# Block ends of a two-layer SSM and attention stack, worked by half rows instead of whole rows

## The reference, cut to what matters

```python
def rmsnorm(x, g):
    y = x32 * lax.rsqrt(jnp.mean(x32 * x32, axis=-1, keepdims=True) + EPS)
    return (y * g).astype(x.dtype)
...
    x = x + rmsnorm(h, mix_post_g[i])          # h: output of the block's last product
    u = rmsnorm(x, mem_pre_g[i])               # u: input of the next block
```

## Time and profile before

| | |
|---|---|
| time, median of 3 runs | 965.77 us (965.77 to 967.42) |
| the profiled execution's own time | 968.91 us |
| its span | 967.1 us |
| TensorE busy | 929.4 us (96%) |
| VectorE busy | 563.3 us (58%) |
| ScalarE busy | 487.8 us (50%) |
| mean granted TensorE clock | 0.987 |

### The profile page before, as it was taken

How to read it: one execution, slowest core, us unless ns; L and a number is a source line. 1 busy time by engine, 2 the same in 40 slices (tenths; PEclk the granted TensorE clock), 3 DMA queues, 4 the chain that set the end, 5 groups by cost and what they waited for, 6 DMA issues and landing times.

```text
span 967.1 us, 15638 instructions
## 1 busy us (share of the span) xinstructions
PE 929.4 (96%) x6624; PEld 860.2 (89%) x6624; DVE 563.3 (58%) x645; ACT 487.8 (50%) x670; POOL 36.1 (4%) x51
## 2 busy tenths in 40 slices
PE   7999999998999989999999999999999599999996
PEld 6999988787899889999988899987998499999885
DVE  6788465784565575455544854675755645554543
ACT  5566467764545564344433554665645534434332
POOL 1000001130000000000000220000000000000000
PEclk9999999999999999999999999999999799999999
DMA  8766442234653365555555697433643345555551
GB/s 261 260 187 192 145 153 89 88 127 138 204 188 128 127 209 187 173 174 186 189 190 189 218 266 220 132 131 131 217 138 115 119 143 191 188 174 174 197 194 44
DMA packets 121061, 163.80 MB, mean 169 GB/s; under 512 B 4076, under 2 KB 106916, under 8 KB 121012
## 3 DMA queue, kind: packets, MB, share of 16 engines
q1 hardware_dynamic: 117684, 151.99, 48.0%
q0 software_dynamic: 3328, 11.10, 3.7%
HBM read 162.01 MB, written 1.07 MB: 169 GB/s over the span
## 4 chain that ended last, share of the span: by engine, by line
PE 84%; DVE 10%; ACT 4%; issue 2%; DMA 1%; SPq 0%; DVEq 0%; ACTq 0%
PE bank L443 76%; DVE w_lo L1152 2%; DVE ntmp L1215 1%; PE bank L750 1%; PE bank L721 1%; DVE x L1218 1%; DVE ntmp L1194 1%; ACT ntmp L861 1%; PE bank L639 1%; PE bank L545 1%; DMA pre_row<-in_mix_pre_g_dram 1%; DVE stats L1183 1%; DVE stats L1185 1%; PE bank L805 1%; PE bank L677 0%
## 5 line engine op out<-in xcount | busy, mean ns | idle before, releaser
L1152 DVE TENSOR_TENSOR w_lo<-w_raw,w_hi 128x2048 fp32r<-128x2048 f32 x135 | 308.4, 2290 | 219.4 <-ACT w_hi L839 219.2
L443 PE MATMUL bank<-actT_hi,w_hi 128*128 128x256 f32 x1280 | 364.8, 285 | 4.8 <-DVE w_lo L1163 1.7
L443 PE MATMUL bank<-actT_lo,w_hi 128*128 128x256 f32 x1280 | 363.2, 284 | 0.0
L443 PE MATMUL bank<-actT_hi,w_lo 128*128 128x256 f32 x1280 | 363.1, 284 | 0.0
L839 ACT ACTIVATE w_hi<-w_raw 128x2048 fp32r<-128x2048 f32 x135 | 256.6, 1907 | 98.6 <-DMA w_raw<-in_ffn_w_down_dram 52.9
L443 PEld LDWEIGHTS bank<-actT_hi,w_hi 128*128 128x128 f32 x1280 | 246.7, 193 | 6.8 <-issue 4.6
L443 PEld LDWEIGHTS bank<-actT_lo,w_hi 128*128 128x128 f32 x1280 | 246.8, 193 | 0.1
L443 PEld LDWEIGHTS bank<-actT_hi,w_lo 128*128 128x128 f32 x1280 | 246.7, 193 | 0.0
L443 PE MATMUL bank<-w_hi,hT_hi 128*128 128x512 f32 x176 | 68.5, 389 | 0.0
L443 PE MATMUL bank<-w_lo,hT_hi 128*128 128x512 f32 x176 | 68.5, 389 | 0.0
L443 PE MATMUL bank<-w_hi,hT_lo 128*128 128x512 f32 x176 | 68.5, 389 | 0.0
(11 more groups left out here) (209 smaller groups left out, 1280.5 us busy)
## 6 DMA issues: line engine op xcount, KB each, us to landing
w_raw<-in_ffn_w_gu_dram SPq DMA_DIRECT2D x44, 1024.0 KB, 5.0
w_raw<-in_ffn_w_down_dram SPq DMA_DIRECT2D x22, 1024.0 KB, 4.9
w_raw<-in_ssm_w_in_dram SPq DMA_DIRECT2D x20, 1024.0 KB, 5.3
w_raw<-in_mem_w_kv_dram SPq DMA_DIRECT2D x16, 1024.0 KB, 5.6
w_raw<-in_ssm_w_out_dram SPq DMA_DIRECT2D x8, 1024.0 KB, 4.9
w_raw<-in_mem_w_q_dram SPq DMA_DIRECT2D x8, 1024.0 KB, 5.1
w_raw<-in_mem_w_o_dram SPq DMA_DIRECT2D x8, 1024.0 KB, 4.9
w_raw<-in_w_kv_dram SPq DMA_DIRECT2D x8, 1024.0 KB, 5.6
```

The source lines that it names most:

```text
L443: ins = pe.matmul(dst, a, b, start=first and n == 0, stop=last and n == len(passes) - 1, skip_group_check=True)
L1152: dve.tensor_tensor(lo[:, s, :], raw[:, s, :], hi[:, s, :].bitcast(F32), ALU.subtract).then_inc(w_lo_done, 1)
```

## The change

- **Last product.** The last two units are run by quarters: for each row tile, for each column half, both units' matmuls of that half (12 matmuls). `m_quarter` is raised after each of the first three quarters, `w_used` of both units only within the fourth.
- **Statistics.** `statistic_halves` squares each half when it is there, with a sum of its own; the first sum goes through one more small activation (scale by 1/1024, plus eps), and Ln takes it as its bias. For x the halves are waited for one by one. `w_hi` of unit `last` + 3 now stands behind all four statistics.
- **Update.** h times the gain row is formed by halves ahead of the norm (`gains`, from the bank), one before and one after the second half's sum. Then one operation for each half gives x = h·gain × norm + x. The two whole-row operations L1215 and L1218 are gone.
- **Next norm and transposes.** `normalise` writes two halves, TensorE waits for each half on its own. This holds for the first turn and the memory's turn too.
- **Weights on VectorE.** `w_lo` of unit `last` + 2 stands after the update of t = 1 instead of t = 0; that of `last` + 3 stands in `turn`, between the two row tiles.
- **Output.** Each half row tile is stored by a DMA of its own (four instead of two).

```diff
             def m_part(name, act_hi, act_lo, ready, last_y=None):
...
+                for t in range(ST):
+                    for half in range(2):
+                        for i in (n - 2, n - 1):
+                            if t == 0 and half == 0:
+                                ready(i)
+                                pe.wait_ge(w_lo_done, U[(name, i)] + 1)
+                            for r in range(MR):
+                                ins = part(i, t, half, r)
+                            if t and half:
+                                ins.then_inc(w_used, 1)
+                        if not (t and half):
+                            ins.then_inc(m_quarter, 1)
...
-                    pe.wait_ge(u_ready, 2 * k + t + 1)
                     for half in range(2):
+                        pe.wait_ge(u_ready, 4 * k + 2 * t + half + 1)
...
+            def statistic_halves(c, t, src, first, second):
+
+                for half, (s, count) in enumerate((first, second)):
+                    cols = slice(half * 512, half * 512 + 512)
+                    act.wait_ge(s, count)
+                    act.activation(ntmp[:, t, cols], src[:, cols], ACT.Square,
+                                   accum_out=stats[:, 0 if half else 6, c:c + 1]).then_inc(sum_ready, 1)
+                    act.wait_ge(sum_ready, sums_in(c, half))
+                    if half == 0:
+                        own.mark(act.activation(stats[:, 7, c:c + 1], stats[:, 6, c:c + 1], ACT.Identity, bias=eps_col, scale=1.0 / D))
+                own.wait()
+                own.mark(act.activation(stats[:, 1, c:c + 1], stats[:, 0, c:c + 1], ACT.Ln, bias=stats[:, 7, c:c + 1], scale=1.0 / D))
+                own.wait()
+                act.activation(stats[:, 2, c:c + 1], stats[:, 1, c:c + 1], ACT.Exp, scale=-0.5).then_inc(stat_ready, 1)
...
-                statistic(stat_col(n, 1, 0), 1, msum[1])
+                statistic_halves(stat_col(n, 1, 0), 1, msum[1], (m_quarter, 3 * n + 3), (w_used, last + 1))
+                if POST_TURN[n] is not None:
+                    statistic_halves(stat_col(n, 1, 1), 1, x[:, 1, :], (x_ready, 4 * n + 3), (x_ready, 4 * n + 4))
                 hi_upto(units_ahead(n))
...
+                    own.mark(dve.tensor_scalar(v0, total0, -0.5 / D, -0.5 * EPS, ALU.mult, ALU.add))
+                    if gains:
+                        gains(0)
+                    dve.wait_ge(sum_ready, sums_in(c, 1))
+                    own.wait()
+                    own.mark(dve.tensor_scalar(v, total, -0.5 / D, v0, ALU.mult, ALU.add))
+                    if gains:
+                        gains(1)
...
+            def turn(k, dst_hi, dst_lo, ahead=-1):
                 for t in range(ST):
+                    if t:
+                        lo_upto(ahead)
                     for half in range(2):
...
-                    own.mark(dve.scalar_tensor_tensor(out=ntmp[:, t, :], in0=msum[t], scalar=stats[:, 5, c:c + 1],
-                                                      in1=post_row[:], op0=ALU.mult, op1=ALU.mult))
-                    own.wait()
-                    dve.tensor_tensor(x[:, t, :], x[:, t, :], ntmp[:, t, :], ALU.add).then_inc(x_ready, 1)
-                    if units_ahead(n) > last_unit(M_OF_POST[n]) + 2:
-                        lo_upto(units_ahead(n) if t else last_unit(M_OF_POST[n]) + 2)
...
+                        own.mark(dve.tensor_tensor(ntmp[:, t, cols], bank[:, 4 + 2 * t + half, :], post_row[:, cols], ALU.mult))
...
+                        dve.scalar_tensor_tensor(out=x[:, t, cols], in0=ntmp[:, t, cols], scalar=stats[:, 5, c:c + 1],
+                                                 in1=x[:, t, cols], op0=ALU.mult, op1=ALU.add).then_inc(x_ready, 1)
+                    if t and units_ahead(n) > last_unit(M_OF_POST[n]) + 2:
+                        lo_upto(last_unit(M_OF_POST[n]) + 2)
```

More of the change, by code:

```diff
@@ L335, in stat_col, with sums_in @@
             return 4 + 4 * n + (2 * t + after if POST_TURN[n] is not None else t)
+        def sums_in(c, half):
+            return c + 1 if c < 4 else 2 * (c - 4) + 5 + half
         def last_unit(name):
@@ L510, in m_part @@
                 n = last_unit(name) - U[(name, 0)] + 1
[L512 to L531, removed]
@@ new lines, in part @@
+                def part(i, t, half, r):
+                    u, k = U[(name, i)], i * MR + r
+                    ah, al = act_hi[:, k, t * P:(t + 1) * P], act_lo[:, k, t * P:(t + 1) * P]
+                    cols = slice(r * D + half * 512, r * D + half * 512 + 512)
+                    wh, wl = hi[:, u % SLOTS, cols], lo[:, u % SLOTS, cols]
+                    return product(bank[:, 4 + 2 * t + half, :], [(ah, wh), (ah, wl), (al, wh)], k == 0, k == n * MR - 1)
+                for i in range(n - 2):
+                    ready(i)
+                    pe.wait_ge(w_lo_done, U[(name, i)] + 1)
+                    for t in range(ST):
+                        if t and i == 0 and last_y:
+                            last_y()
+                        for r in range(MR):
+                            for half in range(2):
+                                ins = part(i, t, half, r)
+                    ins.then_inc(w_used, 1)
@@ L1174, in tiles, with inverse_rms @@
                 return bank[:, b, :].rearrange("p (c n) -> p c n", n=S)
[L1176 to L1180, removed]
+            def inverse_rms(c, gains=None):
+                total, _, r, v, step, result, total0, _, v0 = [stats[:, n, c:c + 1] for n in range(9)]
+                dve.wait_ge(sum_ready, sums_in(c, 0))
+                if c < 4:
+                    own.mark(dve.tensor_scalar(v, total, -0.5 / D, -0.5 * EPS, ALU.mult, ALU.add))
+                else:
+                    own.mark(dve.tensor_scalar(v0, total0, -0.5 / D, -0.5 * EPS, ALU.mult, ALU.add))
[6 more added lines that the diff above has]
+                        gains(1)
                 own.wait()
@@ L1193, in normalise @@
                     dve.wait_ge(*((pre_loaded, 16 * k) if k else (pre_first, 16)))
-                dve.scalar_tensor_tensor(out=ntmp[:, t, :], in0=src[:, t, :], scalar=stats[:, 5, c:c + 1],
-                                         in1=pre_row[:], op0=ALU.mult, op1=ALU.mult).then_inc(u_ready, 1)
-            def turn(k, dst_hi, dst_lo):
+                for half in range(2):
+                    cols = slice(half * 512, half * 512 + 512)
+                    dve.scalar_tensor_tensor(out=ntmp[:, t, cols], in0=src[:, t, cols], scalar=stats[:, 5, c:c + 1],
+                                             in1=pre_row[:, cols], op0=ALU.mult, op1=ALU.mult).then_inc(u_ready, 1)
+            def turn(k, dst_hi, dst_lo, ahead=-1):
                 for t in range(ST):
+                    if t:
+                        lo_upto(ahead)
                     for half in range(2):
@@ L1375, in _ @@
             update(0)
-            turn(2, actT_hi, actT_lo)
+            turn(2, actT_hi, actT_lo, units_ahead(0))
             def memory_attention(layer):
@@ L1430, in _ @@
             update(1)
-            turn(3, actT_hi, actT_lo)
+            turn(3, actT_hi, actT_lo, units_ahead(1))
             lo_upto(U[("gu0", 0)] + 1)
@@ L1434, in _ @@
             update(2)
-            turn(4, actT_hi, actT_lo)
+            turn(4, actT_hi, actT_lo, units_ahead(2))
             for t in range(ST):
@@ L1483, in _ @@
             update(3)
-            turn(6, actT_hi, actT_lo)
+            turn(6, actT_hi, actT_lo, units_ahead(3))
             memory_attention(1)
```

35 lines of the change are left out of this document (17 added, 18 removed).

## The result

The changed kernel takes **967.28 us** (median of 20 runs, 965.95 to 969.46), the kernel before 965.9 us (20 runs, 963.96 to 967.85). The ratio is 1.0015, with a 95% interval of 1.0008 to 1.0022. The forecast was 963.4 us. The change gains at the block ends, somewhat more than was forecast there, and loses it in the large products, by a slowdown that has nothing to do with the new order of work.

The account below looks back on a forecast made before the run. TensorE, busy 929.4 of 967.1 us, was taken as the bound, leaving only its idle time at block ends and the tail. Terms 0.7 − 0.3 − 1.3 − 1.8 + 0.3 = −2.4 us from 965.77 gave 963.4, range 960.8 to 966.7.

Parts of the forecast that it names:

- Elsewhere: Outside the block ends: memory's turn +0.3 us; start, matmuls (same in number) and later weight load nothing.
- four signs of being wrong: `ntmp` wait left at ends with fills, fused operation near 1.3 us, `w_hi` waiting for `w_raw`, clock 1.00 through end 4.
- Ends 0, 2, 3: Block ends with fills: `w_lo` wait replaces `ntmp` wait, about 0.5 us for `actT_lo`; +0.2 us each, +0.7 together.
- new wait for `w_lo`: Ends 0, 2, 3, ahead of the half fill: TensorE waits 1.25 us for unit `last` + 2, replacing the old 1.32.
- Ends 1 and 4: End 1: copy wait hides late pieces, −0.3 us; end 4, without fill: halves shorten the chain, clock still falls, −1.3.
- End 5: Last end: 3.6 us from last half's square instead of 4.83, last store 0.6 us shorter; −1.8 us in all.
- The fused operation: Update of x, two float32 operands from SBUF: priced at full rate, 0.75 us for a half.
- rival 4: Fused operations at half rate, each half 0.53 us more: +6.1 us, 969.5 us; chance 0.02.
- 1: Rival: clock does not fall at end 4, −2.9 us more, 960.5 us; chance 0.10.
- rival 2: Moved weight units eat the gain: VectorE's chain to `w_lo` 0.8 us later at four ends, +3, about 966; chance 0.20.
- Rival 3: Unit `last` + 3 lands late at ends 0, 2, 3, holding `w_hi`, copies and TensorE: 967.7 us; chance 0.07.
- Memory's turn: Normalising by halves ahead of the dt chain, where TensorE already waits 0.33 us for `w_lo`: +0.3 us.

Follow-up runs that it names:

- b_stats9: Kernel before with only the `stats` tile enlarged from 6 to 9 rows, shifting everything behind it 384 bytes: 971.52 us, ratio 1.0046.
- a_phase128: Changed kernel with the phase region moved by 128 bytes, back at its old distance from the weight slots: 963.42 us, ratio 0.9963 to the kernel before.
- experiment 3: Kernel before, phase region moved 128 bytes: 971.39 us; changed kernel, weights and following tiles moved 128 bytes: 966.76, or with everything on multiples of 256: 962.67.
- experiment 1: The run `b_stats9`: kernel before with only `stats` enlarged, 971.52 us against 966.75; end 1 lasted 15.90 us instead of 16.06.
- experiment 5: Changed kernel with the phase region at its old alignment and the block ends' weight units back in their old places: 961.9 us, ratio 0.9951.

## Why the prediction was wrong, point by point

- **The step that failed** is in "Elsewhere": the matmuls are the same in number, so I counted them at the same speed. They cost 4.25 us more, at a term that I had put at nothing. The cause shown is the placement: `b_stats9` makes the kernel before slow by 4.8 us without a changed instruction, `a_phase128` takes 3.9 off the changed one (967.28 to 963.42), or 5.0 by the ratios to before (1.0015 and 0.9963). The hunk was in the diff, and I did not ask what lies behind `stats`. None of the four signs of being wrong that I had named appeared, either: a sum that looks at the block ends alone cannot give one for the products.
- **Of TensorE's operands** the Trainium skill, TensorE: Matmul & The Clock Gate, section Step-by-step: what each phase is for, says that loading the next tile's weights does not take read bandwidth from the running matmul. What the runs show does not sit well with that: two read operands at 128 modulo 256 from each other cost 5.6 ns in each 512-column matmul ((61.34 − 59.87) / 263). That the two reads collide is my reading. The products read nothing else from SBUF, and the other engines' work makes no difference (experiment 3), but no run takes one of the two reads away.
- **Ends 0, 2, 3**: the new wait for `w_lo` in place of the old one came, forecast 1.25 and measured 0.89 to 0.92 (1.04 in `a_phase128`). The 0.5 us for the last `actT_lo` pieces did not, and with it the sign of the term was wrong: +0.7 forecast, −0.72 measured, of which −0.34 is left in `a_phase128`, with the placement put right. The stage was forecast at 14.97 and measured at 14.53 to 14.55 (14.66 to 14.67 in `a_phase128`). Too high were the two small operations ahead of the gain products, 0.36 us in my count and 0.07 and 0.12 in the rows below, and the half square, 0.59 from a bank and 0.62 from x instead of 0.65.

Timeline of VectorE in the changed kernel, end 0, t = 1:

```profile
263.58 0.15 DVE L1210 TENSOR_SCALAR stats<-stats 128x1 f32<-128x1 f32 x1
263.65 0.68 DVE L1259 TENSOR_TENSOR ntmp<-bank,post_row 128x512 f32<-128x512 f32 x1
264.44 0.21 DVE L1215 TENSOR_SCALAR stats<-stats 128x1 f32<-128x1 f32 x1
264.56 0.68 DVE L1259 TENSOR_TENSOR ntmp<-bank,post_row 128x512 f32<-128x512 f32 x1
...
265.79 1.42 DVE L1264 SCALAR_TENSOR_TENSOR x<-ntmp,stats,x 128x512 f32<-128x512 f32 x2
267.12 2.29 DVE L1179 TENSOR_TENSOR w_lo<-w_raw,w_hi 128x2048 fp32r<-128x2048 f32 x1
...
271.66 1.28 DVE L1243 TENSOR_TENSOR actT_lo<-bank,actT_hi 128x512 fp32r<-128x512 f32 x2
272.86 2.28 DVE L1179 TENSOR_TENSOR w_lo<-w_raw,w_hi 128x2048 fp32r<-128x2048 f32 x1
275.06 1.28 DVE L1243 TENSOR_TENSOR actT_lo<-bank,actT_hi 128x512 fp32r<-128x512 f32 x2
```

The order is the one worked out: with E at 261.86, the unit `last` + 2 is done at 7.55 (7.85 forecast) and the last pieces at 14.5 (14.80). From 263.58 on the engine has hardly a gap, and the one wait of TensorE is for this `w_lo`. So at these ends it is now VectorE that sets the time, though without the last `actT_lo` piece TensorE would have begun the next block only 0.15 us earlier (276.24 for 276.39).

- **Ends 1 and 4**: right, −0.41 for −0.3 (−0.26 by the end of the fills, the rest as in experiment 1) and −1.57 for −1.3. The clock did fall at end 4, as I had left it.
- **End 5**: right, −1.96 for −1.8. Against the earlier trace rows:

```profile
960.07 0.60 ACT L880 ACTIVATE ntmp<-bank 128x512 f32<-128x512 f32 x1 [1.76 <-PE bank L449]
960.57 0.19 ACT L880 ACTIVATION_READ_ACCUMULATOR ntmp<-bank 128x1 f32 x1
960.79 0.29 ACT L886 ACTIVATE stats<-stats 128x1 f32<-128x1 f32 x1
961.12 0.20 ACT L888 ACTIVATE stats<-stats 128x1 f32<-128x1 f32 x1
```

```profile
960.93 0.68 DVE L1259 TENSOR_TENSOR ntmp<-bank,post_row 128x512 f32<-128x512 f32 x1
...
962.14 1.41 DVE L1264 SCALAR_TENSOR_TENSOR x<-ntmp,stats,x 128x512 f32<-128x512 f32 x2
```

From the square's start to the last of x 3.48 us (3.6 forecast), and a store of half the size lands in 2.1 instead of 2.6 us, as counted from the earlier trace rows:

```profile
out_dram<-x SPq DMA_DIRECT2D x4, 256.0 KB, 2.1
```

- **The fused operation**: 0.75 us for each half, as taken (0.749 in the mean of 24). The rule of half throughput that the Trainium skill states (Vector Engine (DVE) Microarchitecture Reference, section Points that are easy to get wrong) is not borne out, and rival 4 falls with it.
- **Rivals**: 1, 2 and 4 did not come as priced. The moved weight units of rival 2 do cost something, 0.7 us by the ends of experiment 5, but they did not eat the gain. Rival 3 named a real thing, the later load, but not one that costs in the changed order; only experiment 5 made it visible. None of the four held the case that came.
- **Memory's turn**: TensorE's wait there went from 0.33 to 0.75 us, the stretch up to it longer by 0.2, for +0.3.

With the placement put right the time is in the forecast range: 963.42 us, and 962.2 by the ratio on 965.77. That it falls on the 963.4 of the forecast is luck: the kernel before took 966.75 beside it, so the change is −3.3 us for a forecast of −2.4, and the difference is about what ends 0, 2 and 3 were mis-sized by (+0.7 forecast, −0.34 measured). What stays open: by stages the changed kernel should lose 0.5 us (−1.1 of the spans, without the −1.06 at the start and the −0.53 of clock), and the medians say that it loses 1.4; one profiled execution each does not resolve the rest.

## What to carry to other kernels

A diff that enlarges a buffer moves everything placed behind it. Where addresses are handed out in sequence, list which tiles move, and against which others they are read; for matmuls like these pin the large operands of one matmul at distances of a multiple of 256 bytes, and give small tables their room at the end. When an engine's busy time grows with the same instruction count, compare the spacing of equal instructions far from the edit before explaining anything near it. And a unit of work that is moved out of a chain's way is late for whoever waited for it: here it changed one stall of 1.3 us into one of 0.9 to 1.0.

## What the runs showed of the hardware

In these float32r matmuls (stationary 128 × 128, streamed 128 × 512) the start-to-start time was 226.8 ns at distance 0 modulo 256 between activation tiles and weight slots, 229 at 192, 232.4 at 128 and 233.3 at 32 and 64 (stage down0 less the 0.23 of its last matmul, over its 263 intervals). Moving both together changed nothing. For 32 and 64 the distance was set by the activation tiles' address alone. The matmuls that stream 256 columns, in the gate and up stretch, took 126.81 us in every kernel; there the distance of weights and `actT` was never varied.
